# Expert values in a sparse batch: gathers of half rows, five half rows of V and three slot rows in flight

## The reference

```
s = jnp.einsum('nhcd,hckd->nhck', q, sub_keys)
sv, si = lax.top_k(s, PEER_TOPK)
...
experts = jnp.take_along_axis(cidx, top_p, axis=-1)
gate = jax.nn.softmax(top_s, axis=-1)
act = jax.nn.gelu(jnp.einsum('nd,nhkd->nhk', h, u[experts]))
return jnp.einsum('nhk,nhkd->nd', (gate * act), v[experts])
```

## Time and profile before

| | us |
|---|---|
| three runs | 4479.19, 4491.2, 4501.01 |
| median | 4491.2 |
| the profiled execution, its own time | 4485.46 |
| its span, first to last instruction | 4483.4 |
| mean granted clock of TensorE | 0.980 |

### The profile page before, as it was taken

The page is one execution under the profiler, slowest core; times in us unless marked ns, Lnnn a source line. Parts: engine busy times, 40 slices in busy tenths (PEclk is TensorE's granted clock), DMA queues, the critical chain, the costliest instruction groups (busy, mean ns, idle before and its releaser), DMA issues.

```text
span 4483.4 us, 67360 instructions
## 1 busy us (share of the span) xinstructions
PE 4286.2 (96%) x28423; PEld 4045.4 (90%) x28423; DVE 2951.2 (66%) x4428; ACT 1219.0 (27%) x1614; POOL 652.0 (15%) x680
## 2 busy tenths in 40 slices
PE   7999999999999989999999999999898999989997
PEld 7999888998899979888999999999898888888997
DVE  3232453322434366899999898898677777777887
ACT  3221442332212121232222222222222222222323
POOL 1010002331000000000111111111122232222110
PEclk9999999999999999999999999999999999999998
DMA  6433225775344533355899999999888888888884
GB/s 196 113 105 96 78 89 189 243 244 185 104 133 126 156 75 77 85 126 126 218 285 287 273 291 277 284 283 279 287 310 308 330 344 326 319 317 328 300 294 151
DMA packets 590156, 968.31 MB, mean 216 GB/s; under 512 B 142865, under 2 KB 405009, under 8 KB 547608
## 3 DMA queue, kind: packets, MB, share of 16 engines
q1 hardware_dynamic: 508560, 519.33, 41.0%
q0 software_dynamic: 75776, 434.18, 26.2%
q10 hardware_dynamic: 5520, 10.49, 0.8%
HBM read 873.63 MB, written 85.75 MB: 214 GB/s over the span
## 4 chain that ended last, share of the span: by engine, by line
PE 75%; DVE 13%; DMA 7%; issue 2%; ACT 2%; SPq 1%; ACTq 0%; POOL 0%; DVEq 0%
PE pair L1940 28%; PE pair L2281 21%; PE pair L2358 14%; DMA v_raw<-in_peer_v_dram 6%; PE quad L1940 2%; PE pair L2316 2%; DVE w_lo L1620 2%; DVE s_sum L1799 1%; DVE v_lo L1778 1%; PE pair L1904 1%; PE quad L2340 1%; PE quad L1904 1%; DVE turned L1615 1%; PE quad L2111 1%; DVE main L1805 1%
## 5 line engine op out<-in xcount | busy, mean ns | idle before, releaser
L2281 PE MATMUL pair<-act_hi,w_hi 128*128 128x448 f32 x2048 | 760.3, 371 | 13.7 <-DVE w_lo L1620 13.7
L2358 PE MATMUL pair<-wx_hi,v_hi 128*128 128x384 f32 x2016 | 691.5, 343 | 73.4 <-issue 58.5
L2281 PE MATMUL pair<-act_hi,w_lo 128*128 128x448 f32 x2048 | 751.0, 367 | 0.0
L2281 PE MATMUL pair<-act_lo,w_hi 128*128 128x448 f32 x2048 | 750.9, 367 | 0.0
L1940 PE MATMUL pair<-act_hi,w_hi 128*128 128x288 f32 x3264 | 718.2, 302 | 29.7 <-DVE act_lo L1325 12.7
L1265 DVE TENSOR_TENSOR w_lo<-w_raw,w_hi 128x2048 fp32r<-128x2048 f32 x103 | 236.1, 2292 | 741.1 <-ACT w_hi L869 741.1
L1940 PE MATMUL pair<-act_hi,w_lo 128*128 128x288 f32 x3264 | 701.3, 297 | 0.0
L1940 PE MATMUL pair<-act_lo,w_hi 128*128 128x288 f32 x3264 | 700.4, 297 | 0.0
L2358 PE MATMUL pair<-wx_hi,v_lo 128*128 128x384 f32 x2016 | 685.9, 340 | 0.0
L2358 PE MATMUL pair<-wx_lo,v_hi 128*128 128x384 f32 x2016 | 685.6, 340 | 0.0
L1940 PEld LDWEIGHTS pair<-act_hi,w_hi 128*128 128x128 f32 x3264 | 525.6, 190 | 68.3 <-issue 61.5
(11 more groups left out here) (327 smaller groups left out, 5372.5 us busy)
## 6 DMA issues: line engine op xcount, KB each, us to landing
w_raw<-in_peer_u_dram SPq DMA_DIRECT2D x512, 256.0 KB, 5.8
v_raw<-in_peer_v_dram SPq DMA_DIRECT2D x256, 512.0 KB, 6.9
w_raw<-in_w_in_dram SPq DMA_DIRECT2D x64, 1024.0 KB, 7.3
gelu_dram<-tmp SPq DMA_DIRECT2D x128, 224.0 KB, 7.7
gmat_dram<-gmat SPq DMA_DIRECT2D x48, 512.0 KB, 11.0
a_back<-gelu_dram SPq DMA_DIRECT2D x128, 192.0 KB, 5.4
g_back<-gmat_dram SPq DMA_DIRECT2D x64, 384.0 KB, 6.5
w_raw<-in_w_out_dram SPq DMA_DIRECT2D x16, 1024.0 KB, 7.2
```

The costliest lines, as they stand in the source:

```text
L2281: op = m_(pair[0][:, n % 2, 0:TU], w[n % 2][:, k, :], x[:, k, 0:TU], start=(k == 0 and i == 0), stop=(k == KD - 1 and i == 2))
L2358: op = m_(bank(d), w[:, c], x[:, :], start=(start and t == terms[0]), stop=(stop and t == terms[-1]))
```

## The change

Four things change in the last stage, and all engines' lists move with them.

1. The expert rows are gathered as halves of 1024 columns (`v_half_rows`, 0.5 MB each, `e_row` holds twice the row's number plus the half). A batch has two quarters q = 2 b and 2 b + 1, one for each half; a quarter is 8 matmuls. `SP_STEP` has 32 entries, every 12 steps. The four tiles `e_rows` are half as large.
2. The room goes to V and to the slots: `V_RAWS` is 5 and three slot rows are in flight (`S_RING`). GpSimd waits for slot i - 3.
3. `SUMS` is at d = 3, 7, 11, 15, and the low parts at d = 1, 2, 4, 5 and 9, 10, 12, 13.
4. `ROWS_AT` has three parts per quarter, each behind one slot addition: two half rows, two half rows, then the cells of the next batch (odd quarters) or the weights (even quarters).

```
-SP_STEP = [divmod(2 * KD + 4 + 24 * b, KD) for b in range(SP_N)]
+SP_STEP = [divmod(2 * KD + 4 + 12 * q, KD) for q in range(2 * SP_N)]
-V_RAWS = 3
-SUMS = sorted([(g, d) for g in range(1, N_VG - 1) for d in (4, 7, 12, 15)] + [(g, 6) for g in (5, 12, 19, 26)])
+V_RAWS, S_RING = 5, 3
+SUMS = sorted([(g, d) for g in range(1, N_VG - 1) for d in (3, 7, 11, 15)] + [(g, 6) for g in (5, 12, 19, 26)])
-ROWS_AT = {min(i for i, x in enumerate(SUMS) if x > SP_STEP[b]) + 2 + j: (b + 1, j) for b in range(SP_N - 1) for j in range(5)}
+LOW_AT = (1, 2, 4, 5)
+ROWS_AT = {min(i for i, x in enumerate(SUMS) if x > SP_STEP[q]) + S_RING + k: (q + 1, k) for q in range(2 * SP_N - 1) for k in range(3)}
...
-            for i in range(2, PK + 2):
+            for i in range(S_RING, PK + S_RING):
                 if i < PK:
-                    pool.wait_ge(s_done, S_DONE + i - 1)
+                    pool.wait_ge(s_done, S_DONE + i - S_RING + 1)
                     gather_slot(i)
                 if i in ROWS_AT:
-                    b, j = ROWS_AT[i]
-                    if j == 0:
-                        pool.wait_ge(e_mm, b)
-                    if j < COLS:
-                        gather_row(b, j)
-                    if j == 1 and b + 1 < SP_N:
-                        gather_cells(b + 1)
-                    if j == 4 and b + 1 < SP_N:
-                        weigh(b + 1)
+                    q, k = ROWS_AT[i]
+                    if k == 0:
+                        pool.wait_ge(e_mm, q)
+                    if k < 2:
+                        gather_row(q, 2 * k)
+                        gather_row(q, 2 * k + 1)
+                    elif q % 2 and 2 <= q // 2 + 1 < SP_N:
+                        gather_cells(q // 2 + 1)
+                    elif q % 2 == 0 and q >= 4:
+                        weigh(q // 2)
...
-            def expert_sums(b):
+            def expert_sums(q):
+                b, half = divmod(q, 2)
                 pe.wait_ge(e_wval, b * 2 + 2)
                 for j in range(COLS):
-                    pe.wait_ge(e_in[j], 16 * (b + 1) + U_IN)
-                for c in range(4):
+                    pe.wait_ge(e_in[j], 16 * (q + 1) + U_IN)
+                for c in range(2):
                     for j in range(COLS):
-                        op = m_(pair[2 + c // 2][quadrant(j), c % 2, :], e_w[b % 2][:, j, :],
+                        op = m_(pair[2 + half][quadrant(j), c, :], e_w[b % 2][:, j, :],
                                 e_rows[j][:, c * 512:(c + 1) * 512], start=(b == 0), stop=True, skip_group_check=True)
```

More of the change, by code:

```diff
@@ L292, in hybrid_step @@
         r = Region(A_X, END)
-        e_rows = [r("e_rows0", [P, D])]
+        e_sums = Region(A_X, END)("e_sums", [P, D])
+        e_rows = [r(f"e_rows{s}", [P, D // 2]) for s in range(2)]
         back_at = r.at - BASE
@@ L298, in hybrid_step @@
         e_cell = r("e_cell", [P, N_CELL], U32)
+        e_row = r("e_row", [P, 2, N_CELL], U32)
         rows_at = r.at - BASE
-        e_rows += [r(f"e_rows{s}", [P, D]) for s in (1, 2)] + [e_row3]
-        s_rows = [r(f"s_rows{s}", [P, D]) for s in range(2)]
+        e_rows += [r(f"e_rows{s}", [P, D // 2]) for s in (2, 3)]
+        s_rows = [r(f"s_rows{s}", [P, D]) for s in range(S_RING)]
         r = Region(A_X + 2 * T * 4, back_at)
@@ L339, in hybrid_step @@
         v_rows = peer_v.rearrange("l e d -> (l e) d")
+        v_half_rows = peer_v.rearrange("l e (h d) -> (l e h) d", h=2)
         v_tiles = peer_v.rearrange("l (i j) d -> (l i) j d", j=PK)
@@ L430, in hybrid_step @@
         dot_done, DOT = x_scaled, 2 * TB
-        u_row_in, e_in, s_in = kp_in[0:U_RING], vp_in, kp_in[2:4]
+        u_row_in, e_in, s_in = kp_in[0:U_RING], vp_in, kp_in[1:1 + S_RING]
         U_IN = 16 * DB * PAGES // K_RING
-        S_IN = (U_IN + 16 * len(range(2, N_SU, U_RING)), U_IN)
+        S_IN = [U_IN + 16 * len(range(j, N_SU, U_RING)) * (j < U_RING) for j in range(1, 1 + S_RING)]
         s_done, S_DONE = x_scaled, 2 * TB + N_SU
@@ L620, in _ @@
             load_v(3)
-            load_v(4)
+            load_v(5)
+            load_v(6)
             store_gelu(N_U - 2)
@@ L626, in _ @@
             sp.wait_ge(a_done, N_U)
+            load_v(4)
             load_weights(1)
-            for i in (5, 6, 7):
+            for i in (7, 8, 9, 10):
                 load_v(i)
             load_weights(2)
-            for i in (8, 9):
+            for i in (11, 12):
                 load_v(i)
             load_weights(3)
-            load_v(10)
             for g in range(1, N_VG):
@@ L788, in gather_cells, with gather_row @@
                                             ).then_inc(back_in[b % 4], 16)
-            def gather_row(b, j):
+            def gather_row(q, j):
+                b, half = divmod(q, 2)
                 t = batch_tokens(b)[j]
-                pool.indirect_dma_start(out=e_rows[j][:, :], out_offset=None, in_=v_rows,
-                                        in_offset=bass.IndirectOffsetOnAxis(ap=e_row[:, t:t + 1], axis=0)
+                pool.indirect_dma_start(out=e_rows[j][:, :], out_offset=None, in_=v_half_rows,
+                                        in_offset=bass.IndirectOffsetOnAxis(ap=e_row[:, half, t:t + 1], axis=0)
                                         ).then_inc(e_in[j], 16)
             def gather_slot(i):
-                pool.indirect_dma_start(out=s_rows[i % 2][:, :], out_offset=None, in_=v_rows,
+                pool.indirect_dma_start(out=s_rows[i % S_RING][:, :], out_offset=None, in_=v_rows,
                                         in_offset=bass.IndirectOffsetOnAxis(ap=e_slot[:, i:i + 1], axis=0)
-                                        ).then_inc(s_in[i % 2], 16)
+                                        ).then_inc(s_in[i % S_RING], 16)
             def weigh(b):
@@ L816, in _ @@
                 pool.wait_ge(a_out[s], 16 * N_U // 2)
-            for i in range(2):
+            for i in range(S_RING):
                 gather_slot(i)
-            gather_cells(0)
+            for b in range(2):
+                gather_cells(b)
             for j in range(COLS):
                 gather_row(0, j)
-            gather_cells(1)
             for b in range(2):
                 weigh(b)
-            for i in range(2, PK + 2):
+            for i in range(S_RING, PK + S_RING):
                 if i < PK:
-                    pool.wait_ge(s_done, S_DONE + i - 1)
+                    pool.wait_ge(s_done, S_DONE + i - S_RING + 1)
                     gather_slot(i)
                 if i in ROWS_AT:
-                    b, j = ROWS_AT[i]
-                    if j == 0:
-                        pool.wait_ge(e_mm, b)
-                    if j < COLS:
-                        gather_row(b, j)
-                    if j == 1 and b + 1 < SP_N:
-                        gather_cells(b + 1)
-                    if j == 4 and b + 1 < SP_N:
-                        weigh(b + 1)
+                    q, k = ROWS_AT[i]
[8 more added lines that the diff above has]
+                        weigh(q // 2)
             pool.wait_ge(k_out, 32 * H)
@@ L1180, in take_expert_sums @@
             def take_expert_sums():
-                act.wait_ge(e_mm, SP_N)
+                act.wait_ge(e_mm, 2 * SP_N)
                 for i in range(2):
-                    a.copy(e_rows[0][:, i * D // 2:(i + 1) * D // 2], pair[2 + i][:, :, :].rearrange("p a c -> p (a c)")).then_inc(e_taken, 1)
+                    a.copy(e_sums[:, i * D // 2:(i + 1) * D // 2], pair[2 + i][:, :, :].rearrange("p a c -> p (a c)")).then_inc(e_taken, 1)
             act.wait_ge(dot_done, DOT + N_SU)
@@ L1202, in _ @@
                 after = V_GROUPS[g + 1] if g + 1 < N_VG else ()
[L1203 to L1214, removed]
+                for half, ns in ((1, V_GROUPS[g]), (0, after)):
+                    for n in ns[0:2]:
+                        value_high(V_AT[n, half])
+                    for n in after[0:2] if half else after[2:4]:
+                        weight_high(n)
+                    for n in ns[2:4]:
+                        value_high(V_AT[n, half])
                 if g == SP_LAST:
@@ L1765, in _ @@
             dve.wait_ge(gm_mm, N_G)
-            cell, col = iaT[:, 0:N_CELL], iaT[:, N_CELL:2 * N_CELL]
+            cell, col, row = (iaT[:, i * N_CELL:(i + 1) * N_CELL] for i in range(3))
             link(v.scalar_tensor_tensor(cell, ibT[:, TV:TU], float(P), iaT[:, TV:TU], ALU.mult, ALU.add),
                  v.tensor_scalar_add(col, iota_f[:, 0:N_CELL], float(TV)),
+                 v.scalar_tensor_tensor(row, iaT[:, TV:TU], float(P), ibT[:, TV:TU], ALU.mult, ALU.add),
                  v.tensor_copy(e_gate[:, :], gT[:, TV:TU]))
+            for half in range(2):
+                link(v.tensor_scalar(e_row[:, half, :], row, 2.0, float(half), ALU.mult, ALU.add))
             v.scalar_tensor_tensor(e_cell[:, :], cell, float(TU), col, ALU.mult, ALU.add).then_inc(top_done, 1)
@@ L1792, in add_slot @@
             def add_slot(i):
```

(8 more changed lines are left out.)

14 lines of the change are left out of this document (4 added, 10 removed).

## The result

| | before | changed |
|---|---|---|
| median of the runs, us | 4496.1 | 4678.4 |
| lowest to highest | 4479.2 to 4502.5 | 4672.8 to 4680.9 |
| profiled execution, us | 4485.5 | 4680.3 |
| mean granted clock of TensorE | 0.980 | 0.961 |

The ratio is 1.041, with a 95% interval from 1.038 to 1.044: slower by 182 us. The forecast was 4620 us, with a range from 4550 to 4690.

What follows compares the result with a forecast made beforehand. TensorE's own work and its waits bound the kernel; 29 x (5.2 + 2.2) + 3 = 218 us added at the expert sums, 89 taken away with V's waits, +129 us: 4620 us, range 4550 to 4690.

Steps and rivals of the forecast that it cites:

- what the change takes away: Expert value product: V's waits 59.4 us, lost clock 27 us there and 3 us after, together -89 us.
- the weights' wait: Ahead of 13 even expert sums: weights (e_w) made one step before due, 4.5 us, overlapping the wait for rows.
- The clock: After each gap at an expert sum TensorE runs at 1.2 GHz for a stretch, losing 2.2 us.
- 29 x 5.2 + 3: Waits for half rows ahead of expert sums: 5.2 us at 29 of 31 later sums, 3 us at one.
- waits of 8 us: Sign at the expert sums: waits of 2 or 8 us would show the forecast wrong in size.
- V no longer hurries while TensorE stands: Reason at the expert sums for taking a 5.2 us wait, between 4.2 at the fastest and 6.1 at the median.
- One sum a lead of nine steps (no wait): Additional slot additions at step 6 of groups 5 and 12 give one expert sum nine steps' lead, no wait.
- one of six (3 us): The same additional slot additions give one expert sum a lead of six steps, with a 3 us wait.
- the rows come faster than a whole row did: Rival at the expert sums: half rows land 5.3 us after issue, odd sums wait 2.5 us; 4521 us, chance 0.11.
- V's waits stay: Rival at the value matmuls: DMA share of 0.86 binds the waits, not the ring; +218, 4709 us, chance 0.06.
- it gets faster: Rival at the expert sums: gathers land inside the four steps, only the weights' 59 us remain; 4461 us, chance 0.03.
- no measurable change: Rival at the expert sums: waits shorter than in the first rival, V's waits partly left; chance 0.03.

## Why the prediction was right, and where it was off

**The mechanism** was right, point by point. V's waits went (73.4 to 1.2 us of gaps ahead of value matmuls), and a new wait stands ahead of the expert sums because the half rows are asked for too late. With rows and weights early, what the change takes away is left over: the prediction had worked out 89 us, and that run is 94 us below the kernel before, median against median (98 in the stage). The 3.1 us from a step's end to the next gather, the weights' wait (4.5, measured 4.4, at 13 sums) and its being hidden behind the rows are shown by the chain and by three runs. The clock was forecast at 2.2 us per wait; 66.3 us over 31 waits are 2.1.

**The size** was off by 58 us against the median. By the terms of the sum:

| us | predicted | measured |
|---|---|---|
| waits ahead of the sums | 154 | 220.9 |
| clock lost behind them | 64 | 66.3 |
| taken away with V's waits | -89 | -101 (what is left of the stage's 186.6) |
| together | 129 | 186.6 |

So the mis-sized term is "29 x 5.2 + 3": 31 waits, 7.1 us each (7.9 at odd sums, 6.4 at even ones), where its upper bound was 6.1. The gain was put 12 us too small, which hid part of it. The measured 4678 us lies above the 4655 that the prediction's own bounds give (it writes 4665 further down, which no sum of it gives) and below 4690 only because the range was drawn past them by judgement: that it lies inside is partly luck. By the prediction's own sign, waits of 8 us, the size was wrong at the odd sums. Two of the term's steps failed.
- "V no longer hurries while TensorE stands." In the windows of two waits the DMA engines are at 1.0, 401 and 379 GB/s, where the mean before was 0.86. So it is before all 31 of these sums: from the last slot gather's start to the last landing the share is 0.98 to 1.03. V's loads behind the last low parts, the end of the weights' loads and of the half rows asked for at s+3, the slot gather and the last half rows all fall in the same 12 us. At the odd sum at 3523.95 us, 3.0 MB went through GpSimd's queue (q0) and 2.2 MB through SP's (q1) in the 13 us after the slot gather's start:

```profile
q0 software_dynamic: 606, 3.01, 58.0%
q1 hardware_dynamic: 631, 2.16, 44.6%
```

  The last half row landed 9.7 us after its issue at the median, against 10.1 for a whole one, though it stands one issue (1.25 us) further behind:

```profile
v_raw<-in_peer_v_dram SPq DMA_DIRECT2D x186, 512.0 KB, 7.9
...
e_rows<-in_peer_v_dram,e_row POOLq DMA_INDIRECT x124, 9.7
s_rows<-in_peer_v_dram,e_slot POOLq DMA_INDIRECT x97, 6.5
```

- "One sum a lead of nine steps (no wait)", the sum of quarter 5. It waited 7.7 us. The two additions at steps 6 and 7 of group 5 come right after each other, so GpSimd asks for two slots and four half rows within nine us, and the last of them lands 14 us after its issue (the sum with "one of six (3 us)", quarter 14, waited 4.7):

```profile
3429.58 0.95 POOL s_rows L803
...
3434.55 1.30 POOL s_rows L803
...
3437.75 14.04 DMA e_rows<-in_peer_v_dram,e_row
...
3451.93 3.64 PE quad L2334 x16
```

So each wait should have been costed by the bytes in both queues from the first gather on, at the rate of full engines, and not by the mean of the stage. The last half row as a term by itself, with the median of a different neighbourhood, came out 2 us short per sum. That the full engines set the landing is read from the trace; no run took V's loads out of these 12 us, and with a ring of three the waits stayed as they were.

One count of the prediction is off without weight: it gives the expert sums 32 times 8 matmuls, "the same 512". The program has 8 for a half and 256 in all; the trace records 16 for a half (x16) and 512 in all, before and after.

**The rivals.** That the rows come faster than a whole row did was wrong: 13 us passed from the slot gather to the last landing of the 2.1 MB at an odd sum, and 11.5 at an even one. The Trainium skill (DMA: Bandwidth & Descriptors, Anatomy of one DMA) fits one DMA as 2.0 us plus bytes over 436 GB/s, which gives an estimated 6.8 us for these bytes. The trace does not agree, and the measurement decides; here two queues share engines at a share of 1.0. That V's waits stay was wrong, by ScalarE's 1.2 us. That it gets faster was wrong, and so was no measurable change. The kernel with the rows at once is faster, but not as that rival had it: its rows don't land faster, they are asked for earlier. The last half row has 10 to 18 us from its issue to the sum, where the changed kernel leaves it 2.8.

## What to carry to other kernels

When a transfer is cut in halves over the same buffers, its lead is cut as well: count the steps between the last request and its use, and compare them with all the bytes that both queues must move in that time, at the rate of full engines (here about 400 GB/s), not with a mean landing time. That is read from this trace, not tried ahead of a run. Place a gather on the event that frees its buffer, not behind the next addition that happens to pace the queue. And when two waits hide each other, take both away before judging either: the ring of five was worth at most 10 us with one order and 100 with the other.

## What the runs showed that I had not expected

- Full DMA engines for 12 us at a time beside a mean share of 0.73, and 1 us of idle time in 924 at a mean share of 0.94. The mean share told neither.
- The last 0.5 MB gather of a quarter (9.7 us) landed about as late as the last 1 MB one of a batch before (10.1) in the same queue, so its own size says little. With the half rows ahead of the slot gather the first of the four landed 4.5 us after its issue at the median, and the last one at odd sums still 8.8.
- Moving slot additions by one step (4 and 12 instead of 3 and 11) cost 78 us, through the list of an engine that is busy 40% of the stage.
